# Context tiles normalized and turned during the second gated network's down product, and taken ahead of x by the first joint block

## The chip, the cores and the metric

The kernel runs on one core of a Trainium2 chip. The metric is the device time of one execution in microseconds, and the time of a kernel is the median of its runs. Engine names are those of the profile: PE is TensorE (PEld its weight loads), DVE VectorE, ACT ScalarE, POOL GpSimd, SP SyncE, which issues the loads of the weights.

## What is computed

`reference` is two blocks in a row on 256 tokens x 1024 features, all in float32. The first has two layers (a mixer, cross attention to a memory, and a gated feed-forward network each). The second has two joint layers: x (256 tokens) and a context (256 tokens) are each normalized and modulated, projected by one weight to queries, keys and values, and attend together; then a mixture of experts follows. The stretch that matters here is the end of the first block's second layer and the beginning of the second block's first:

```python
x = x + swiglu(rmsnorm(x, norm_ffn[l]), ffn_w_gu[l], ffn_w_down[l])     # l = 1
...
xc = ctx                                                                # not touched so far
mod  = (silu_c  @ w_ada[i] + b_ada[i])[:, None, :]                      # i = 0
modc = (silu_cc @ w_ada[i] + b_ada[i])[None, None, :]
sh_a, sc_a, ...  = jnp.split(mod, 6, axis=-1)
shc_a, scc_a, ... = jnp.split(modc, 6, axis=-1)
h  = _modulate(_rmsnorm(x,  g_attn[i]), sh_a,  sc_a)                    # 256 x 1024
hc = _modulate(_rmsnorm(xc, g_attn[i]), shc_a, scc_a)                   # 256 x 1024
q, k, v    = _split_qkv(h,  w_qkv[i])                                   # 1024 x 1536
qc, kc, vc = _split_qkv(hc, w_qkv[i])
```

So `hc` needs nothing of the first block, and `h` needs all of it.

## The kernel before

Each engine has its own program, written out by hand in the order in which it runs; semaphores tie them together. Nothing reorders it.

Tokens are cut into tiles of 128: tiles 0 and 1 are x, 2 and 3 the context (both in `xs`). A dense product goes in slots: one slot is a weight block of 1024 rows (8 pieces of 128; 6 in some slots of the down product) by 512 columns, kept in one of four ring buffers. Float32 is done in three products of a rounded format: both the activations and the weights are split into a high part and what is left (low part), and high x high, high x low and low x high are summed. Weight blocks are split by ACT (`split`, L1295, the high part into another ring buffer) and DVE (L1740, the low part in place), a slot ahead (`ahead`). A unit is one tile by one slot, 24 products of 128x512 into one PSUM bank (18 for a slot of six pieces). PE signals `w_used` as it begins a slot, and SP then issues the load that takes the buffer set free.

An activation tile is made ready by `norm`: DVE sums the squares (L1721), POOL raises the mean square to the power -0.5 (L2655), DVE multiplies by that and by the scale row in `bc` slot 0 (L1769) and adds the shift row of slot 1 (L1772) into `hb`; PE turns it with eight 128x128 transposes into banks T0 and T1 (L687), ACT copies each bank as the high part (L1280) and DVE subtracts for the low part (L1727). T0 and T1 must be free of that before the next tile is turned. The scale and shift rows are fetched by POOL (`fill`) from a scratch tensor that POOL's `modulation(0)` wrote in the linear attention; one fill has to wait until the rows before it in the same buffer were used (`normed`).

The down product of the gated network (`ff_out1`, within `feed_forward`) has six slots by two tiles: three slots into banks 0 and 1, three into banks 2 and 3. Its activations `ff_T` take the first 11264 columns of the 12288-column `arena`. Then `joint(0)` follows: two ada blocks (condition vector by modulation weights, L665, for the layer after), both x tiles and both context tiles normalized, with high parts in `hT` and low parts (`LO_J`) in the last 4096 columns of the arena; then slot 0 of `qkv0` on tiles 0, 1, 2, 3, slot 1 on the same, two more ada blocks, the turning of queries, and slot 2. ACT reads out the even tiles (L1376) and DVE the odd ones (L1920). The context itself was loaded by POOL in `cross(1)`.

## Time and profile before

| what | value |
|---|---|
| median of 3 runs | 2543.71 us (2541.72 to 2549.36) |
| the profiled execution | 2542.04 us, span 2540.2 us |
| PE busy | 2137.8 us, 84% of the span |
| DVE, ACT, POOL busy | 1087.4, 681.5, 262.3 us |
| mean granted clock of PE | 0.922 of full |

The page cuts the span in 40 slices of 63.5 us. Two expert stages (slices 21 to 29 and 32 to 40, roughly) have the DMA engines busy in nine tenths and DVE in one tenth; elsewhere PE is the busy one and DMA has room. The stretch between the end of the second gated network's up product (about 932 us) and the second pair of ada blocks in the joint layer (1067 us) lies in slices 15 to 17. In the timelines, a row merges instructions of one form that follow each other; its "idle before" is the time in which the engine did nothing ahead of it, with the instruction that ended it. In a table by stretch, a granted clock of 1.00 is 2.4 GHz and 0.50 is 1.2 GHz.

### The profile page before, as it was taken

To read this page: it belongs to the slowest core of one execution; us is meant where nothing else is said; L and a number is where in the kernel's file an instruction comes from. 1 tells how busy PE (TensorE), PEld (TensorE's weight loads), DVE (VectorE), ACT (ScalarE), POOL (GpSimd) and SP (SyncE) were. 2 spreads that over 40 slices of the span, in tenths; PEclk is the share of its full clock that TensorE was granted. 3 is DMA by queue.
4 is the path that set the end of the run, shared out by engine and by line. 5 is a ranking of instruction groups with operands and counts; after the bars stand their busy time and mean duration, and the time that the engine had idled before them with its cause. 6 is when DMAs were issued, how large, how long until landed. Compare 5 with 4: busy or idle time off the path is not lost. (4 is left out here: it accounts for less than half of the span.)

```text
span 2540.2 us, 29357 instructions
## 1 busy us (share of the span) xinstructions
PE 2137.8 (84%) x11338; PEld 1358.5 (53%) x11338; DVE 1087.4 (43%) x1713; ACT 681.5 (27%) x1048; POOL 262.3 (10%) x392
## 2 busy tenths in 40 slices
PE   6889999996999997987979888888568698888884
PEld 5777787784777876764733333333355433333331
DVE  5667644545676545467531111111576411111112
ACT  3343434332333432246211011111316111111111
POOL 2010000100000000000211111111120111111110
PEclk9989999997999998999979999999779799999997
DMA  8745565551655646310489999999810889999994
GB/s 278 266 144 203 181 211 191 202 200 67 236 199 182 217 173 216 110 35 1 189 354 396 409 413 406 410 404 382 276 25 1 311 356 408 422 415 413 413 414 188
DMA packets 175984, 655.24 MB, mean 258 GB/s; under 512 B 17680, under 2 KB 63200, under 8 KB 150544
## 3 DMA queue, kind: packets, MB, share of 16 engines
q1 hardware_dynamic: 157888, 618.45, 63.7%
q0 software_dynamic: 16752, 32.20, 3.9%
q10 hardware_dynamic: 1248, 3.25, 0.3%
q8 instruction: 68, 1.11, 0.2%
q14 instruction: 28, 0.23, 0.0%
HBM read 653.64 MB, written 21.17 MB: 266 GB/s over the span
## 5 line engine op out<-in xcount | busy, mean ns | idle before, releaser
L651 PE MATMUL bank<-sb_ring_rounded,sb_hT_rounded 128*128 128x512 f32 x2672 | 675.5, 397 | 18.9 <-DVE sb_hT_rounded L1727 12.2
L1185 PE MATMUL bank<-sb_ring,sb_arena 128*64 128x512 f32 x1984 | 507.4, 659 | 129.5 <-DMA sb_ring<-in_w_up 126.7
L651 PEld LDWEIGHTS bank<-sb_ring_rounded,sb_hT_rounded 128*128 128x128 f32 x2672 | 506.0, 191 | 128.5 <-DVE sb_hT_rounded L1727 14.1
L1740 DVE TENSOR_TENSOR sb_ring_rounded<-sb_ring,sb_ring_rounded 128x2048 fp32r<-128x2048 f32 (+1 forms) x148 | 328.2, 2259 | 133.1 <-ACT sb_ring_rounded L1295 132.8
L1185 PEld LDWEIGHTS bank<-sb_ring,sb_arena 128*64 128x64 f32 x1984 | 155.9, 150 | 426.4 <-issue 418.9
L1295 ACT ACTIVATE sb_ring_rounded<-sb_ring 128x2048 fp32r<-128x2048 f32 (+1 forms) x148 | 271.7, 1886 | 171.1 <-PE bank L651 141.8
L651 PE MATMUL bank<-sb_ring_rounded,sb_arena_rounded 128*128 128x512 f32 x1168 | 312.5, 393 | 2.0 <-DVE sb_arena_rounded L1727 1.0
L651 PEld LDWEIGHTS bank<-sb_ring_rounded,sb_arena_rounded 128*128 128x128 f32 x1168 | 221.1, 190 | 48.8 <-issue 2.6
L1209 PE MATMUL bank<-sb_ring,sb_arena 128*64 128x512 f32 x1024 | 233.7, 598 | 1.7 <-DVE sb_arena L2458 1.7
L1643 ACT ACTIVATE sb_hb<-bank 64x512 f32<-64x512 f32 x64 | 37.8, 590 | 644.6 <-PE bank L1185 644.6
L2458 DVE COPY sb_arena<-bank 128x256 f32<-128x256 f32 x64 | 27.2, 425 | 396.1 <-PE bank L1196 396.0
L2474 DVE COPY sb_arena<-bank 64x512 f32<-64x512 f32 x64 | 44.3, 693 | 231.0 <-PE bank L1185 231.0
L2464 DVE COPY sb_arena<-bank 64x512 f32<-64x512 f32 x64 | 44.3, 693 | 205.6 <-PE bank L1209 205.6
L1209 PEld LDWEIGHTS bank<-sb_ring,sb_arena 128*64 128x64 f32 x1024 | 68.4, 137 | 116.4 <-issue 110.4
L2607 POOL DMA_INDIRECT scratch_y<-sb_arena,sb_pick x64 | 60.2, 941 | 448.1 <-DVE sb_arena L2464 439.2
L1177 PEld LDWEIGHTS bank<-sb_cst,sb_arena 64*128 64x128 f32 x512 | 61.2, 199 | 68.9 <-issue 68.9
L687 PE MATMUL bank<-sb_cst,sb_hb 128*128 128x128 f32 x192 | 32.9, 326 | 74.2 <-DVE sb_hb L2539 22.3
L1634 ACT ACTIVATE sb_arena<-bank 64x512 f32<-64x512 f32 x64 | 37.8, 590 | 195.8 <-PE bank L1209 195.8
L1177 PE MATMUL bank<-sb_cst,sb_arena 64*128 64x64 f32 x512 | 70.0, 278 | 17.9 <-DMA sb_arena<-scratch_tokens,sb_spare 17.9
L2655 POOL TENSOR_TENSOR sb_st<-sb_st,sb_cst 128x1 f32<-128x1 f32 x32 | 28.6, 899 | 542.2 <-DVE sb_st L1722 446.2
L1280 ACT ACTIVATE sb_hT_rounded<-bank 128x512 fp32r<-128x512 f32 x68 | 38.9, 595 | 159.5 <-PE bank L687 156.3
L832 PE MATMUL bank<-sb_cst,sb_hb 128*128 128x128 f32 x320 | 48.9, 296 | 25.1 <-DVE sb_hb L1954 24.4
(315 smaller groups left out, 1955.0 us busy)
## 6 DMA issues: line engine op xcount, KB each, us to landing
sb_ring<-in_w_down SPq DMA_DIRECT2D x64, 2048.0 KB, 22.8
sb_ring<-in_w_up SPq DMA_DIRECT2D x62, 2048.0 KB, 21.8
sb_ring<-in_w_gate SPq DMA_DIRECT2D x62, 2048.0 KB, 17.5
sb_ring<-in_w_ada SPq DMA_DIRECT2D x48, 1024.0 KB, 7.4
sb_ring<-in_ffn_w_gu SPq DMA_DIRECT2D x44, 1024.0 KB, 7.7
sb_ring<-in_xa_w_kv SPq DMA_DIRECT2D x16, 1024.0 KB, 7.3
sb_ring<-in_ffn_w_down SPq DMA_DIRECT2D x16, 1024.0 KB, 6.4
sb_ring<-in_od_w_in SPq DMA_DIRECT2D x12, 1024.0 KB, 6.3
```

Source lines behind the costliest of these rows:

```text
L651: ins = pe.matmul(bank[b][0:rows, :], rnd(x), rnd(w[:, k, :]), start=start and k == k0 and q == 0, stop=stop and k == k1 - 1 and q == len( ...
L832: ins = pe.transpose(bank[T0 + a][:, k * P:(k + 1) * P], j_e[:, m % 2, a, k * P:(k + 1) * P], ident)
L1177: ins = pe.transpose(bank[T0 + j][:, k * ROWS:(k + 1) * ROWS], mx[0:ROWS, j, k:D:KD], ident[0:ROWS, 0:ROWS])
L1185: ins = pe.matmul(bank[2 * j + part][part * ROWS:(part + 1) * ROWS, :], mxT[:, j, k, :], w[:, k, :], start=k == 0, stop=k == KD - 1)
L1209: ins = pe.matmul(bank[S0 + n][n * ROWS:(n + 1) * ROWS, :], mactT[:, j, k, :], w[:, k, n * NB:(n + 1) * NB], start=k == 0, stop=k == 3)
L1280: act.activation(rnd(dst), bank[b][:, 0:n * P].rearrange("p (k n) -> p k n", k=n), ACT.Copy).then_inc(*c.up(s["x_hi"]))
L1295: act.activation(rnd(high_of(n)[:, k0:k1, :]), slot_of(n)[:, k0:k1, :], ACT.Copy).then_inc(*c.up(s["w_hi"]))
L1634: act.activation(my[0:ROWS, j, 0:NB], bank[S0][0:ROWS, :], ACT.Copy).then_inc(m["y_lo"], 1)
L1740: dve.tensor_tensor(rnd(w), w, whole(high_of(n)[:, k0:k1, :]), ALU.subtract).then_inc(*c.up(s["w_lo"]))
L2464: dve.tensor_copy(my[0:ROWS, j, NB:2 * NB], bank[S1][ROWS:P, :]).then_inc(m["y_hi"], 1)
L2474: dve.tensor_copy(mup[0:ROWS, j, :], bank[2 * j + 1][ROWS:P, :]).then_inc(m["up"], 1)
L2607: pool.indirect_dma_start(out=DR["y"][l], out_offset=bass.IndirectOffsetOnAxis(ap=pick[:, 1, j:j + 1], axis=0), in_=my[0:ROWS, j, :], in_o ...
```

## The change

Five things are done.

1. In the down product of layer 1, DVE normalizes both context tiles right behind its first weight split (`norm([2, 3], ..., turn=False)`), PE turns them behind the third slot (`norm(2)` in `feed_forward`), ACT copies their high parts ahead of its fourth further split, and DVE subtracts the low parts behind its two residual additions.
2. POOL fetches the context's scale and shift rows first and x's behind them.
3. The context's high parts now go to columns 0 and 1 of `hT`, its low parts to columns 2 and 3, and x's high and low parts to the arena's last 4096 columns (`HI_QKV0`, `LO_QKV0`), which are free only after the down product.
4. In `joint(0)` slot 0 takes the tiles in the order 2, 3, 0, 1, and x's tiles are turned ahead of its second and third unit. The banks read out follow that order.
5. The short row of sinks gets a semaphore of its own, `sink_loaded`, in place of sharing `ctx_loaded`.

The diff, without the hunk that adds `sink_loaded` to the list of semaphores:

```diff
...
@@ -409,9 +409,11 @@
 
         LO2 = (hT, 2)
         LO_J = (view(8192, 2, KD, 2 * P), 0)
+        HI_QKV0 = ((view(8192, KD, 2 * P), 0), (hT, -2))
+        LO_QKV0 = ((view(10240, KD, 2 * P), 0), (hT, 0))
 
         def low(lo, t, k0=0, k1=KD):
-            v, off = lo
+            v, off = lo[t // 2] if isinstance(lo[0], tuple) else lo
             if len(v.shape) == 4:
                 return v[:, t // 2, k0:k1, t % 2 * P:(t % 2 + 1) * P]
             return v[:, k0:min(k1, v.shape[1]), (off + t) * P:(off + t + 1) * P]
@@ -976,6 +978,8 @@
                         ins = unit(b, n0 + q, t, turned(0, q), turned(1, q), q % 3 == 0, q % 3 == 2)
                         if q % 3 == 2:
                             publish(ins, b, "d")
+                    if l == 1 and q == 2:
+                        norm(2)
                 if l == 0:
                     tile_by_tile(n0 + 4, lambda q: turned(0, q + 4), lambda q: turned(1, q + 4), False, ((2, 3), (2, 3)))
 
@@ -1064,13 +1068,19 @@
                 publish(ins, b, "d")
 
             def joint(l):
+                n0 = first[f"qkv{l}"]
                 if l == 0:
                     modulate("qkv0")
-                norm(2)
-                if l == 0:
+                    for u, t in enumerate((2, 3, 0, 1)):
+                        if u in (1, 2):
+                            norm_tile(u - 1)
+                        if u == 3:
+                            hT_settled()
+                        claim(u)
+                        publish(unit(u, n0, t, HI_QKV0, LO_QKV0), u, copy_by(0, t))
+                else:
                     norm(2)
-                hT_settled()
-                n0 = first[f"qkv{l}"]
+                    hT_settled()
 
                 def queries(tiles):
                     for t in tiles:
@@ -1082,10 +1092,10 @@
                         transpose_queries(jq[:, t, 0:D])
 
                 if l == 0:
-                    gemm(n0, 2, [0, 1, 2, 3], copy_by, LO_J)
+                    gemm(n0 + 1, 1, [0, 1, 2, 3], copy_by, LO_QKV0, hi=HI_QKV0)
                     modulate("qkv0_rest")
                     queries(range(4))
-                    gemm(n0 + 2, 1, [0, 1, 2, 3], copy_by, LO_J)
+                    gemm(n0 + 2, 1, [0, 1, 2, 3], copy_by, LO_QKV0, hi=HI_QKV0)
                 else:
                     gemm(n0, 2, [0, 1], copy_by, LO_J)
                     gemm(n0 + 2, 1, [0, 1], copy_by, LO_J)
@@ -1484,6 +1494,8 @@
                         high((T0, T1)[t], ff_T[:, 0, 2 * i:2 * i + 2, t * P:(t + 1) * P], 2)
                 c.next(s["mul_ready"], 2)
                 for q in range(4 if l == 0 else 6):
+                    if l == 1 and q == 3:
+                        norm([2, 3], HI_QKV0)
                     ahead(first[f"ff_out{l}"] + q)
                 if l == 0:
                     tile_by_tile(first["ff_out0"] + 4)
@@ -1540,15 +1552,14 @@
             def joint(l):
                 if l == 0:
                     modulated("qkv0")
-                norm([0, 1])
-                if l == 0:
-                    norm([2, 3])
+                    norm([0, 1], HI_QKV0)
                 else:
+                    norm([0, 1])
                     scale_rows([2, 3])
                 if l == 0:
                     ahead(first["qkv0"])
-                    for t in (0, 2):
-                        project(0, t, t)
+                    for t in (2, 0):
+                        project(0, t, 2 - t)
                     project(1, 0, 0)
                     flag(s["proj_act"])
                     ahead(first["qkv0"] + 1)
@@ -2142,7 +2153,12 @@
                 n0 = first[f"ff_out{l}"]
                 for q in range(3):
                     ahead(n0 + q)
+                    if l == 1 and q == 0:
+                        dve.wait_ge(s["ctx_loaded"], 16)
+                        norm([2, 3], 0, 1, turn=False)
                 residual(None, [(0, t) for t in range(2)])
+                if l == 1:
+                    turned([2, 3], LO_QKV0, HI_QKV0)
                 ahead(n0 + 3)
                 if l == 1:
                     ahead(n0 + 4)
@@ -2234,10 +2250,8 @@
 
             def joint(l):
                 if l == 0:
-                    norm([0, 1], 0, 1, lo=LO_J)
-
-                    dve.wait_ge(s["ctx_loaded"], 32)
-                    norm([2, 3], 0, 1, lo=LO_J)
+                    norm([0, 1], 0, 1, turn=False)
+                    turned([0, 1], LO_QKV0, HI_QKV0)
                 hbf = hb[:].rearrange("p a b -> p (a b)")
                 table = lambda at, t: cst[:, at + HD * t:at + HD * (t + 1)]
 
@@ -2260,13 +2274,14 @@
 
                 if l == 0:
                     ahead(first["qkv0"])
-                    for t in (1, 3):
-                        project(0, t, t)
+                    for t in (3, 1):
+                        project(0, t, 4 - t)
                     project(1, 1, 1)
                     settle()
                     dve.wait_ge(*c.next(s["proj_act"]))
                     for t in range(2):
                         turn_queries(t)
+                    dve.wait_ge(s["sink_loaded"], 16)
                     step(dve.tensor_scalar(nsink, sink1, -1.0, None, ALU.mult))
                     ahead(first["qkv0"] + 1)
                     project(1, 3, 3)
@@ -2738,18 +2753,16 @@
             for l in range(2):
 
                 if l == 0:
-                    fill(0, mod(l, 0, 1))
-                    fill(1, mod(l, 0, 0))
-                    norms()
-                else:
-                    norms()
+                    fill(0, mod(l, 1, 1))
+                    fill(1, mod(l, 1, 0))
+                norms()
                 if l == 0:
                     with nc.allow_non_contiguous_dma(reason="a short row"):
-                        pool.dma_start(sink1, I["sink_a_2"][0].partition_broadcast(P)).then_inc(s["ctx_loaded"], 16)
+                        pool.dma_start(sink1, I["sink_a_2"][0].partition_broadcast(P)).then_inc(s["sink_loaded"], 16)
                 fill(2, mod(l, 0, 2))
                 normed()
-                fill(0, mod(l, 1, 1))
-                fill(1, mod(l, 1, 0))
+                fill(0, mod(l, 1 - (l == 0), 1))
+                fill(1, mod(l, 1 - (l == 0), 0))
                 norms()
                 normed()
                 if l == 0:
```

How the order on DVE changes, from the second split of the down product on. Before: L1740 is a split, L1809 a residual addition, L1721 and L1722 the mean square, L1769 and L1772 the two steps of modulation.

```order
L1740 TENSOR_TENSOR sb_ring_rounded<-sb_ring,sb_ring_rounded 128x2048 x2
L1740 TENSOR_TENSOR sb_ring_rounded<-sb_ring,sb_ring_rounded 128x1536 x2
L1740 TENSOR_TENSOR sb_ring_rounded<-sb_ring,sb_ring_rounded 128x2048 x2
L1809 TENSOR_TENSOR sb_xs<-sb_xs,bank 128x512 x2
L1740 TENSOR_TENSOR sb_ring_rounded<-sb_ring,sb_ring_rounded 128x2048 x2
L1740 TENSOR_TENSOR sb_ring_rounded<-sb_ring,sb_ring_rounded 128x1536 x2
L1740 TENSOR_TENSOR sb_ring_rounded<-sb_ring,sb_ring_rounded 128x2048 x2
L1809 TENSOR_TENSOR sb_xs<-sb_xs,bank 128x512 x2
L1721 ISA sb_hb,sb_st<-sb_xs 128x1024
L1721 ISA sb_st 128x1
L1722 TENSOR_SCALAR sb_st<-sb_st 128x1
```

After, from the same place (the lines are 11 further down: L1751, L1820, L1732, L1733, L1780, L1783; L1738 is the subtraction):

```order
L1751 TENSOR_TENSOR sb_ring_rounded<-sb_ring,sb_ring_rounded 128x2048 x2
L1732 ISA sb_hb,sb_st<-sb_xs 128x1024
L1732 ISA sb_st 128x1
L1733 TENSOR_SCALAR sb_st<-sb_st 128x1
L1732 ISA sb_hb,sb_st<-sb_xs 128x1024
L1732 ISA sb_st 128x1
L1733 TENSOR_SCALAR sb_st<-sb_st 128x1
L1780 SCALAR_TENSOR_TENSOR sb_hb<-sb_xs,sb_st,sb_bc 128x1024
L1783 TENSOR_TENSOR sb_hb<-sb_hb,sb_bc 128x1024
L1780 SCALAR_TENSOR_TENSOR sb_hb<-sb_xs,sb_st,sb_bc 128x1024
L1783 TENSOR_TENSOR sb_hb<-sb_hb,sb_bc 128x1024
L1751 TENSOR_TENSOR sb_ring_rounded<-sb_ring,sb_ring_rounded 128x1536 x2
```

Further down on DVE, after:

```order
L1751 TENSOR_TENSOR sb_ring_rounded<-sb_ring,sb_ring_rounded 128x2048 x2
L1820 TENSOR_TENSOR sb_xs<-sb_xs,bank 128x512 x2
L1738 TENSOR_TENSOR sb_hT_rounded<-bank,sb_hT_rounded 128x4x128 x4
L1751 TENSOR_TENSOR sb_ring_rounded<-sb_ring,sb_ring_rounded 128x2048 x2
L1751 TENSOR_TENSOR sb_ring_rounded<-sb_ring,sb_ring_rounded 128x1536 x2
L1751 TENSOR_TENSOR sb_ring_rounded<-sb_ring,sb_ring_rounded 128x2048 x2
L1820 TENSOR_TENSOR sb_xs<-sb_xs,bank 128x512 x2
L1732 ISA sb_hb,sb_st<-sb_xs 128x1024
```

The ten rows of the context's normalization have moved from behind the down product and x's tiles to a place behind the first split, and its four subtractions stand behind the first pair of residual additions.

How the order on PE changes, from the last transposes of the up product to the first slot of the projection. Before: L954 turns the gated activations, L651 is a product, L665 an ada block, L687 a transpose. From the last rows shown on, pairs and single products go on alternating, since high and low parts lie in different tensors.

```order
L954 MATMUL bank<-sb_cst,sb_arena 128x128 x4
L651 MATMUL bank<-sb_ring_rounded,sb_arena_rounded 128x512 x264
L665 MATMUL bank<-sb_ring,sb_silu 32x128 x64
L687 MATMUL bank<-sb_cst,sb_hb 128x128 x32
L651 MATMUL bank<-sb_ring_rounded,sb_hT_rounded 128x512 x2
L651 MATMUL bank<-sb_ring_rounded,sb_arena_rounded 128x512
L651 MATMUL bank<-sb_ring_rounded,sb_hT_rounded 128x512 x2
L651 MATMUL bank<-sb_ring_rounded,sb_arena_rounded 128x512
```

After (L956, L653, L667, L689 are the same four):

```order
L956 MATMUL bank<-sb_cst,sb_arena 128x128 x4
L653 MATMUL bank<-sb_ring_rounded,sb_arena_rounded 128x512 x132
L689 MATMUL bank<-sb_cst,sb_hb 128x128 x16
L653 MATMUL bank<-sb_ring_rounded,sb_arena_rounded 128x512 x132
L667 MATMUL bank<-sb_ring,sb_silu 32x128 x64
L653 MATMUL bank<-sb_ring_rounded,sb_hT_rounded 128x512 x24
L689 MATMUL bank<-sb_cst,sb_hb 128x128 x8
L653 MATMUL bank<-sb_ring_rounded,sb_hT_rounded 128x512 x24
L689 MATMUL bank<-sb_cst,sb_hb 128x128 x8
L653 MATMUL bank<-sb_ring_rounded,sb_arena_rounded 128x512 x96
L653 MATMUL bank<-sb_ring_rounded,sb_hT_rounded 128x512 x48
L667 MATMUL bank<-sb_ring,sb_silu 32x128 x64
```

Of the 32 transposes that stood between the ada blocks and the projection, 16 stand in the middle of the down product's 264 products, and eight each behind the first and the second unit of the projection.

## Rows read from the trace of the kernel before

**Rows 1.** By stretch: its us, then each engine's busy us, granted clock, DMA.

```profile
997.60:1022.20 24.60, 6.96 (x33) 5.61 (x33) 17.71 (x22) 5.79 (x10) 8.25 (x16) 0.58 0.66 238
1022.20:1025.50 3.30, 3.30 (x8) 2.63 (x9) 2.31 (x2) 2.75 (x2) 2.57 (x6) 0.50 0.46 96
1025.50:1067.40 41.90, 41.90 (x186) 34.43 (x184) 14.09 (x15) 6.52 (x8) 0.00 (x0) 1.00 0.26 94
```

**Rows 2.** Timeline of PE: start, us, line, what, count, idle before.

```profile
932.25 61.70 PE L651 MATMUL bank<-sb_ring_rounded,sb_arena_rounded 128*128 128x512 f32 x264 [0.98 <-issue]
993.89 3.70 PE L665 MATMUL bank<-sb_ring,sb_silu 128*32 128x128 f32 x128
1000.42 1.09 PE L687 MATMUL bank<-sb_cst,sb_hb 128*128 128x128 f32 x8 [2.84 <-DVE sb_hb L1772]
1003.57 1.94 PE L687 MATMUL bank<-sb_cst,sb_hb 128*128 128x128 f32 x8 [2.05 <-DVE sb_arena_rounded L1727]
1015.63 1.97 PE L687 MATMUL bank<-sb_cst,sb_hb 128*128 128x128 f32 x8 [10.12 <-DVE sb_hb L1772]
...
1022.18 1.19 PE L651 MATMUL bank<-sb_ring_rounded,sb_hT_rounded 128*128 128x512 f32 x2 [1.46 <-DVE sb_arena_rounded L1727]
...
1067.43 3.70 PE L665 MATMUL bank<-sb_ring,sb_silu 128*32 128x128 f32 x128
```

**Rows 3.** Timeline of DVE, same columns, down product to projection.

```profile
934.77 4.50 DVE L1740 TENSOR_TENSOR sb_ring_rounded<-sb_ring,sb_ring_rounded 128x2048 fp32r<-128x2048 f32 x2 [2.62 <-ACT sb_ring_rounded L1295]
946.78 3.43 DVE L1740 TENSOR_TENSOR sb_ring_rounded<-sb_ring,sb_ring_rounded 128x1536 fp32r<-128x1536 f32 x2 [7.51 <-ACT sb_ring_rounded L1295]
...
988.01 4.49 DVE L1740 TENSOR_TENSOR sb_ring_rounded<-sb_ring,sb_ring_rounded 128x2048 fp32r<-128x2048 f32 x2 [7.88 <-ACT sb_ring_rounded L1295]
...
994.72 1.23 DVE L1721 CUSTOM_DVE_ANT_0 sb_hb<-sb_xs 128x1024 f32<-128x1024 f32 x1
...
1001.60 1.22 DVE L1772 TENSOR_TENSOR sb_hb<-sb_hb,sb_bc 128x1024 f32<-128x1024 f32 x1
...
1023.19 4.49 DVE L1740 TENSOR_TENSOR sb_ring_rounded<-sb_ring,sb_ring_rounded 128x2048 fp32r<-128x2048 f32 x2 [1.11 <-ACT sb_ring_rounded L1295]
```

**Rows 4.** Timeline of POOL, first layer's modulation rows and powers.

```profile
802.90 1.12 POOL L2649 DMA_DIRECT2D sb_bc<-scratch_mod  x2 [1.62 <-DVE sb_hb L1819]
...
1003.12 1.05 POOL L2649 DMA_DIRECT2D sb_bc<-scratch_mod  x2 [3.83 <-DVE sb_hb L1772]
```

**Rows 5.** Timeline of ACT, projection's read-outs and weight split.

```profile
1021.25 3.70 ACT L1295 ACTIVATE sb_ring_rounded<-sb_ring 128x2048 fp32r<-128x2048 f32 x2
...
1040.34 0.60 ACT L1376 ACTIVATE sb_arena<-bank 128x512 f32<-128x512 f32 x1 [10.28 <-PE bank L651]
1051.22 0.60 ACT L1376 ACTIVATE sb_arena<-bank 128x512 f32<-128x512 f32 x1 [10.28 <-PE bank L651]
```

**Rows 6.** Timeline of PE, two earlier places with transposes among products.

```profile
156.48 1.03 PE L687 MATMUL bank<-sb_cst,sb_hb 128*128 128x128 f32 x8
158.58 1.17 PE L687 MATMUL bank<-sb_cst,sb_hb 128*128 128x128 f32 x8 [1.07 <-DVE sb_arena_rounded L1727]
159.50 11.14 PE L651 MATMUL bank<-sb_ring_rounded,sb_hT_rounded 128*128 128x512 f32 x48
...
288.74 1.03 PE L687 MATMUL bank<-sb_cst,sb_hb 128*128 128x128 f32 x8
289.52 10.69 PE L651 MATMUL bank<-sb_ring_rounded,sb_hT_rounded 128*128 128x512 f32 x46
```

**Rows 7.** Loads into the ring between 990 and 1050 us, its last line.

```profile
DMA to landing us min/median/max: 5.2/7.4/16.4
```

**Rows 8.** What SP waited for, 940 to 1330 us: total, times, longest.

```profile
SPq L545 <- PE bank L651: 164.0, 1, 164.0
```

**Rows 9.** Table by stretch as in rows 1, at two places of gaps.

```profile
156.40:159.50 3.10, 2.03 (x19) 1.63 (x16) 1.98 (x3) 1.34 (x3) 0.00 (x0) 1.00 0.00 0
...
934.00:936.00 2.00, 2.00 (x6) 1.57 (x5) 1.23 (x1) 2.00 (x2) 0.00 (x0) 0.50 0.77 270
```

More of the change, by code:

```diff
@@ L175, in build_program @@
             "act_back", "act_go", "act_step", "ctx_loaded", "bcx", "o_split", "dve_step", "e_ready",
-            "es_ready", "fin_ready", "gla_dve", "h_ready", "idx_ready", "logits_read", "in_loaded",
+            "es_ready", "fin_ready", "gla_dve", "h_ready", "idx_ready", "logits_read", "sink_loaded", "in_loaded",
             "marks_ready", "fix_loaded", "mem_loaded", "mod_stored", "raw_stored0", "raw_stored1", "silu_ready", "ms_ready", "mul_ready", "nmax_ready", "out_done",
```

## The prediction

> **What bounds the kernel now.** I read the 40 slices of the page first: up to the first expert stage (about 1270 us) TensorE is busy in eight or nine tenths of nearly every slice while the DMA engines are half idle; in the expert stages the picture is turned round. The changed stretch, 930 to 1100 us, lies in the part that TensorE sets. A table by stage then shows how it is filled [rows 1]: the down product of the gated network and the ada blocks stand without a gap [rows 2], and then 24.60 us follow in which PE works 6.96 us, at a granted clock of 0.58. After it PE is full again, first at 0.50 of its clock, then at 1.00. The timeline of PE names the hole [rows 2]: the last product ends at 993.89, two ada blocks take 3.70 us, then 32 transposes stand in pairs of eight, the first three behind idle times of 2.84, 2.05 and 10.12 us, and the first product of the joint projection starts at 1022.18. Every idle time there is put down to DVE, which normalizes x, turns it, and then does both again for the context.
>
> The timeline of POOL says why 10.12 us are the longest: the context's scale and shift rows are fetched into the buffers that x's rows still fill, so their transfers start at 1003.12, only when x is normalized [rows 4], and after landing and modulation the context's first transpose stands at 1015.63 [rows 2]. The context's own data have been in place since the second cross attention. So the hole depends on order, not on late data.
>
> **What is removed.** I count PE's time from the end of the down product (993.89) to the start of the next ada blocks (1067.43), the same two points of work in both kernels: 73.54 us now [rows 2]. Between them lie 8 units of 24 products. ACT reads every second unit out at 1040.34 and 1051.22, so two units take 10.88 us and one 5.44 at full clock [rows 5]; 8 are 43.52. Now they take 1067.43 - 1022.18 = 45.25, because they begin at half clock.
>
> **What stands there after the change.**
> Two ada blocks: 3.70, unchanged [rows 2].
> Two units on context tiles follow, the first at once, since the context was turned before. Their weights are split by DVE at 988.01 to 992.50 [rows 3], about 8 us before they are wanted, and this moves with PE.
> x's tile 0: now PE could begin to transpose it 1000.42 - 993.89 = 6.53 us after the last product [rows 2]; wanted after 3.70 + 5.44 = 9.14. Covered by 2.6 us. Tile 1 is normalized at 1002.8 (end of the row at 1001.60 [rows 3]), 8.9 us after the last product, wanted at 15.4. Covered by 6.4.
> Each x tile still costs its 8 transposes on PE. Where eight transposes stand in front of products that don't need them, PE goes on after 289.52 - 288.74 = 0.78 us [rows 6]: twice 0.78 is 1.56. Copy and subtraction of the first half are done 158.58 - 156.48 = 2.1 us after the first transpose [rows 6] and lie beside a unit of 5.44.
> Sum from 993.89's point of work: 3.70 + 43.52 + 1.56 = 48.78 us, instead of 73.54: 24.76 us less.
>
> **What is added.** 16 transposes of the context in the down product, behind its third slot (at about 963.9 us), where PE has no gap now. The nearest row is a pair of eight between products at full clock: 156.48 to 159.50, 3.02 us, 1.07 of it idle because the second tile's bank is freed by DVE's subtraction [rows 6]. Lower bound: no wait, 2 x 0.78 = 1.56. Upper bound: the same pair in the hole, 1000.42 to 1005.51, 5.1 us [rows 2]. I take 3.1, the row at full clock with products on either side; DVE is in its last residual addition when the first half is turned, but ACT's copy hides that. ACT does its four copies before the next weight split. That split and DVE's own, 3.70 and 4.50 us by a first and second half that overlap, follow from about 967.5 to 974; PE wants them one slot of 10.88 us after 967.0, at 977.9. Nothing follows from it.
> The context's normalization costs DVE 994.72 to 1002.8, 8.1 us [rows 3]. It is put behind the split that ends at 939.27, so it ends at 947.4; DVE is idle now until 946.78. The split of the 1536-wide piece slips 0.6 us, to end at 950.8. PE wants it at about 955.8: back from 993.9 over slots of 8.16, 10.88 and 10.88 us to 963.9, and 8.16 more. What stands behind the new wait for the context on DVE is this split, and PE behind it; the wait is empty, as POOL issued the rows at 802.90 [rows 4], and POOL itself has nothing in front of its power. Its queue of fills moves with that: x's rows are issued at about 947 and land far ahead of 997.
> The next split (second slot of the projection) is what becomes late next. Now: started by ACT at 1021.25 and done by DVE at 1027.7 [rows 3, 5], 18 us early. Afterwards: ACT is free when it has copied x's tile 1, (993.89 + 3.1) + 3.70 + 5.44 + 0.78 + 5.44 + about 2.2 = 1014.6; DVE's first half ends at 1018.8 and the second at 1021.1; PE wants the first at 997.0 + 3.70 + 21.76 + 1.56 = 1024.0. Covered by 5 us. The weights for it are issued when PE begins the first ada block, then at about 997.4; the slowest load into the ring between 990 and 1050 landed in 16.4 us [rows 7], so by 1013.8, before ACT asks. The slot after it keeps its distance from its load, which PE releases as it begins the second slot.
> The other edits (sink on its own semaphore, other slot numbers of banks) change no duration; the bank order only swaps which of two free banks is read first. I cost them at 0, with 0.3 either way.
>
> **Sum:** 24.76 - 3.1 = 21.7 us. Later stages start when PE arrives: SP's first expert load waits 164.0 us for PE's product [rows 8], and so do the loads before it, so the whole rest moves up. The profiled execution took 2542.04 us (span 2540.20); 2542.04 - 21.7 = 2520.3. It lies 1.7 us below the median 2543.71, which would give 2522.0. I forecast 2522.
>
> **The clock.** At 156.4 to 159.5, eight and eight transposes between products, the granted clock stays 1.00 [rows 9]. But soon after 932.25, behind an idle time of 0.98 us, it is 0.50 [rows 2, 9], and the 264 products take 61.70 us [rows 2] where 59.84 would do (264 x 10.88 / 48): 1.9 us lost. So a fall at the new place is possible and costs up to 1.9 us.
> The Trainium skill (TensorE: Matmul & The Clock Gate, Part 4: PE-mode transpose) says that transposes don't count as work for the clock the way products do. By that rule a fall at the inserted transposes would be the usual case and the forecast 2524; by this trace's row at 156.4 it is the exception.
>
> **Rivals.**
> (a) The clock falls once or twice more, at 964 or at x's tiles: 1.9 to 3.8 us back, 2523.9 to 2525.8. For: 932.2. Against: 156.4 and 288.74, where products went on at full speed.
> (b) A wait takes the hole's place: the second slot's split or x's tile 0 comes later than worked out. x's tile 0 has only 2.6 us of cover. If POOL's answer or x's rows were 5 us later, PE would stand 2.4 us; if the load of the second slot shared its rate with both ada loads and took twice 16.4 us, it would land at 1030, ACT's first half and DVE's be done 4.1 us later at 1034, 10 us late: 2532. Against: all are earlier in every row.
> (c) The gain is given back in the expert stage: if its loads ran at a fixed rate from a fixed moment, nothing of 21.7 us would be left, 2543.7. Against it stands rows 8: the loads start at PE's release.
> (d) Slower than before: the clock falls at the inserted transposes at 964 and stays at 1.2 GHz to the end of the down product. The remaining products take 993.89 - 963.9 = 30.0 us at full clock and 60 at half: +30.0 - 21.7, 2552. It decides from the point where more than 21.7 us worth of products run at half clock. Against: behind the hole, with a gap ten times as long as the one added, the half clock lasted from 1022.2 to 1025.5 only [rows 1].
> The same page (Part 1, Seeing it yourself) warns of clocks seen stuck low for tens of microseconds; no row here shows it.
> (e) The change does not do what it says: the context's rows are not there at 939 and DVE waits. They were issued 136 us before.
>
> **How the numbers follow.** Forecast as worked out 0.71; (a) 0.17; (b) 0.07; (c) and (e) together 0.03; (d) 0.02. The time given is the first's, 2522. Its own range is 2517 to 2526 (1.5 less and 2.0 more for the inserted pair, and the three runs of before spread 7.6 us). To take in (a) and part of (b): 2515 to 2530. A difference of 0.3%, 7.6 us, is about what can be told from none. Forecast, (a) and most of (b) are faster by more, (c) and (e) same, (d) slower: 0.95, 0.03, 0.02.
>
> **What would show it.** Right: 16 transposes at about 964 with some 3 us to the next product; products of the joint projection right behind the ada blocks, about 997.0 + 3.7; two pieces of eight transposes without idle time; no idle time on PE near 10 us there; the second pair of ada blocks starting at about 1045.7 (1067.43 - 21.7). Wrong: an idle time before x's tile 0 above 0.5 us, PE waiting for the weight split at about 1024, a clock of 0.50 after 967, or expert loads that start less than some 21.7 us earlier than now.

## The result and the profile after

| | before | after |
|---|---|---|
| median of 4 runs | 2545.32 us (2541.72 to 2549.36) | 2523.91 us (2520.56 to 2526.08) |
| the profiled execution | 2542.04 us, span 2540.2 | 2525.83 us, span 2524.0 |
| PE busy | 2137.8 us | 2135.7 us |
| start of the down product | 932.25 | 936.72 |
| from there to the second pair of ada blocks | 135.18 | 113.96 |
| from there to the first expert load | 168.02 | 164.30 |
| from there to the end | 1304.75 | 1309.02 |

The ratio is 0.9915, its 95% interval 0.9898 to 0.9932: a gain of 0.7 to 1.0%, clear of none. (The median of before has four runs here; the table ahead of the prediction had three of them.) The median fell by 21.4 us; 21.7 was forecast. Of the four stretches in the table the second is the one that the change touches, and it gave 21.22 us. The other three differ by +4.47, -3.72 and +4.27 us, so that the two profiled executions lie only 16.2 us apart; they are taken up below.

The timeline of PE after the change, with the columns of [rows 2]:

```profile
936.72 31.79 PE L653 MATMUL bank<-sb_ring_rounded,sb_arena_rounded 128*128 128x512 f32 x132 [0.98 <-issue]
968.35 1.04 PE L689 MATMUL bank<-sb_cst,sb_hb 128*128 128x128 f32 x8
970.46 1.16 PE L689 MATMUL bank<-sb_cst,sb_hb 128*128 128x128 f32 x8 [1.07 <-DVE sb_hT_rounded L1738]
971.38 30.18 PE L653 MATMUL bank<-sb_ring_rounded,sb_arena_rounded 128*128 128x512 f32 x132
1001.49 3.70 PE L667 MATMUL bank<-sb_ring,sb_silu 128*32 128x128 f32 x128
1005.12 5.74 PE L653 MATMUL bank<-sb_ring_rounded,sb_hT_rounded 128*128 128x512 f32 x24
1010.70 1.03 PE L689 MATMUL bank<-sb_cst,sb_hb 128*128 128x128 f32 x8
1011.49 5.71 PE L653 MATMUL bank<-sb_ring_rounded,sb_hT_rounded 128*128 128x512 f32 x24
1017.03 1.04 PE L689 MATMUL bank<-sb_cst,sb_hb 128*128 128x128 f32 x8
1017.83 22.05 PE L653 MATMUL bank<-sb_ring_rounded,sb_arena_rounded 128*128 128x512 f32 x96
1039.71 11.04 PE L653 MATMUL bank<-sb_ring_rounded,sb_hT_rounded 128*128 128x512 f32 x48
1050.68 3.70 PE L667 MATMUL bank<-sb_ring,sb_silu 128*32 128x128 f32 x128
```

The transposes of the context stand at 968.35, and 3.03 us later the products go on. Behind the two ada blocks the first unit of the projection begins at once, at 1005.12, where [rows 2] had 24.6 us of transposes and idle time. The two x tiles are the rows of eight at 1010.70 and 1017.03, each 0.79 or 0.80 us ahead of the next product and without idle time. No row between the inserted pair and the second ada pair has an idle time in brackets. The table by stretch, answering to [rows 1], shows PE full and its clock at full speed in each of its four windows between 968 and 1046 us, but for the 1.07 us in which PE waits at the inserted pair:

```profile
968.00:997.00 29.00, 27.93 (x132) 23.09 (x131) 12.57 (x10) 12.03 (x10) 0.00 (x0) 1.00 0.48 166
1001.00:1006.00 5.00, 5.00 (x135) 4.32 (x134) 3.94 (x8) 0.56 (x2) 1.99 (x2) 1.00 0.54 169
1006.00:1024.00 18.00, 18.00 (x89) 15.06 (x88) 10.33 (x10) 6.68 (x8) 6.09 (x13) 1.00 0.92 339
1024.00:1046.00 22.00, 22.00 (x99) 18.22 (x98) 8.36 (x10) 5.33 (x7) 0.00 (x0) 1.00 0.27 95
```

The timeline of DVE gives the normalization of the context (first and last row), the split that had to wait for it, the end of x's tile 0 and the split of the second slot:

```profile
943.88 1.22 DVE L1732 CUSTOM_DVE_ANT_0 sb_hb<-sb_xs 128x1024 f32<-128x1024 f32 x1
...
950.76 1.23 DVE L1783 TENSOR_TENSOR sb_hb<-sb_hb,sb_bc 128x1024 f32<-128x1024 f32 x1
951.90 3.42 DVE L1751 TENSOR_TENSOR sb_ring_rounded<-sb_ring,sb_ring_rounded 128x1536 fp32r<-128x1536 f32 x2
...
1006.74 1.22 DVE L1783 TENSOR_TENSOR sb_hb<-sb_hb,sb_bc 128x1024 f32<-128x1024 f32 x1
...
1020.59 4.49 DVE L1751 TENSOR_TENSOR sb_ring_rounded<-sb_ring,sb_ring_rounded 128x2048 fp32r<-128x2048 f32 x2 [1.01 <-ACT sb_ring_rounded L1305]
```

The context is ready at 951.99; the split of the 1536-wide piece starts as the last step ends, and is done at 955.32, about 5 us before PE begins that slot (968.35 less the 8.16 us of a slot of six pieces). x's tile 0 is ready at 1007.96 and PE asks for it at 1010.70. The split ends at 1025.08, while PE's fifth unit starts at about 1028.8 (1039.71 less two units of 5.44). The next two views are ACT's splits of the second and the third slot, the latter with a wait of 1.75 us for its load (1.90 in the kernel before), and POOL's power and fetch of x's rows:

```profile
1018.64 3.73 ACT L1305 ACTIVATE sb_ring_rounded<-sb_ring 128x2048 fp32r<-128x2048 f32 x2
...
1037.06 3.72 ACT L1305 ACTIVATE sb_ring_rounded<-sb_ring 128x2048 fp32r<-128x2048 f32 x2 [1.75 <-DMA sb_ring<-in_w_qkv]
```

```profile
945.39 1.99 POOL L2670 TENSOR_TENSOR sb_st<-sb_st,sb_cst 128x1 f32<-128x1 f32 x2 [136.88 <-DVE sb_st L1733]
...
952.28 1.05 POOL L2664 DMA_DIRECT2D sb_bc<-scratch_mod  x2 [3.83 <-DVE sb_hb L1783]
```

### The profile page after: what moved, and what is told of

Its sections match the earlier page's. It is cut to its first block and busy times, and to the rows that moved or that the text cites. A ratio compares the mean times of both kernels' runs of the same rounds, so it can differ in the third digit from the quotient of the medians.

```text
span 2524.0 us, 29358 instructions
## 1 busy us (share of the span) xinstructions
PE 2135.7 (85%) x11338; PEld 1357.3 (54%) x11338; DVE 1086.6 (43%) x1713; ACT 681.3 (27%) x1048; POOL 262.4 (10%) x392
## 5 line engine op out<-in xcount | busy, mean ns | idle before, releaser
L653 PE MATMUL bank<-sb_ring_rounded,sb_hT_rounded 128*128 128x512 f32 x2624 | 650.6, 398 | 17.4 <-DVE sb_hT_rounded L1738 12.2
L653 PEld LDWEIGHTS bank<-sb_ring_rounded,sb_hT_rounded 128*128 128x128 f32 x2624 | 497.5, 192 | 125.6 <-DVE sb_hT_rounded L1738 14.1
L1751 DVE TENSOR_TENSOR sb_ring_rounded<-sb_ring,sb_ring_rounded 128x2048 fp32r<-128x2048 f32 (+1 forms) x148 | 328.1, 2258 | 125.9 <-ACT sb_ring_rounded L1305 125.6
L653 PE MATMUL bank<-sb_ring_rounded,sb_arena_rounded 128*128 128x512 f32 x1216 | 308.9, 393 | 2.0 <-issue 2.0
L653 PEld LDWEIGHTS bank<-sb_ring_rounded,sb_arena_rounded 128*128 128x128 f32 x1216 | 229.9, 190 | 50.6 <-issue 2.6
L689 PE MATMUL bank<-sb_cst,sb_hb 128*128 128x128 f32 x192 | 30.2, 307 | 60.4 <-DVE sb_hb L2554 23.5
```

Of the source, the lines that this page charges most:

```text
L653: ins = pe.matmul(bank[b][0:rows, :], rnd(x), rnd(w[:, k, :]), start=start and k == k0 and q == 0, stop=stop and k == k1 - 1 and q == len( ...
L1751: dve.tensor_tensor(rnd(w), w, whole(high_of(n)[:, k0:k1, :]), ALU.subtract).then_inc(*c.up(s["w_lo"]))
```

## The experiments

Each cut of a diff below shows the part of the edit that matters; what has to follow it on the other engines (copies, subtractions, the order in which banks are read out) is left out.

All comparisons of stages use the stretch from the down product's first product to the second pair of ada blocks, called the stretch. It is read from the traces; its spread for one kernel is 0.05 us for three traces after the change (113.96, 114.01, 113.96) and 0.3 for four before (135.18, 135.50, 135.34, 135.46; what varies is the landing of the context's rows, with PE waits of 10.12 to 10.60 us). Medians of whole runs spread far more, as the last two parts show.

**The two halves of the change.** `x_first` keeps the early context and undoes the order of slot 0:

```diff
-                    for u, t in enumerate((2, 3, 0, 1)):
-                        if u in (1, 2):
-                            norm_tile(u - 1)
-                        if u == 3:
-                            hT_settled()
+                    norm(2)
+                    hT_settled()
+                    for u, t in enumerate((0, 1, 2, 3)):
```

> The changed kernel, but slot 0 of the joint projection takes x's tiles first and the context's behind them, both x tiles being turned ahead of the first unit, as before the change. The context is still normalized and turned in the down product. Theory (two things make the gain, the early context and the order of the tiles, which hides x's normalization and turning behind units on context tiles): PE waits for x's tile 0 until 6.5 us after the last product, turns the pair in 5.1, waits 1.5 more: first product 13.1 us after the last one instead of 3.6, less 1.6 for the transposes saved between units, 7.9 us more than the changed kernel, and up to 1.9 more if the clock falls: 2532 to 2534. Rival (the hole was above all the 10 us wait for the context's rows, so that the early context alone brings nearly all): within 3 us of the changed kernel, 2524 to 2527.

Measured: the stretch 123.92 us, median 2531.66 (2530.68 to 2536.72; ratio to before 0.9946, 0.9925 to 0.9968). PE's timeline there, and the clock of the first products behind it:

```profile
1001.14 3.70 PE L667 MATMUL bank<-sb_ring,sb_silu 128*32 128x128 f32 x128
1007.67 1.09 PE L689 MATMUL bank<-sb_cst,sb_hb 128*128 128x128 f32 x8 [2.83 <-DVE sb_hb L1781]
1010.82 1.94 PE L689 MATMUL bank<-sb_cst,sb_hb 128*128 128x128 f32 x8 [2.06 <-DVE sb_arena_rounded L1736]
1014.22 13.52 PE L653 MATMUL bank<-sb_ring_rounded,sb_arena_rounded 128*128 128x512 f32 x48 [1.46 <-DVE sb_arena_rounded L1736]
```

```profile
1014.20:1017.00 2.80, 2.78 (x7) 2.22 (x8) 1.78 (x1) 2.79 (x2) 2.60 (x6) 0.50 0.82 229
```

PE waits 2.83, 2.06 and 1.46 us, the clock falls to 0.50, and the 48 products of x's tiles, a row of 13.52 us, take 2.4 us more than a row of 48 at full clock (11.1). The first product stands 13.08 us after the first ada block instead of 3.63, less 1.59 for the two rows of eight that the changed kernel has between units: 7.9 us of waiting and transposing. The other 2.1 us are in the eight units, 46.08 us here and 43.97 in the changed kernel, and come with the lower clock. The stretch is 9.96 us longer than the changed kernel's; 7.9 to 9.8 was expected. The rival is out.

`ctx_late` undoes the early context and keeps the order (beside the turning in the joint block, as in `turn_late` below):

```diff
-                    if l == 1 and q == 0:
-                        dve.wait_ge(s["ctx_loaded"], 16)
-                        norm([2, 3], 0, 1, turn=False)
...
                 if l == 0:
+                    dve.wait_ge(s["ctx_loaded"], 16)
+                    norm([2, 3], 0, 1, turn=False)
+                    turned([2, 3], LO_QKV0, HI_QKV0)
                     norm([0, 1], 0, 1, turn=False)
```

> The changed kernel without the early context: it is normalized and turned in the joint block, ahead of x, and slot 0 still takes the context's tiles first. With the kernel that had the early context but x first, this makes a square of two by two. Theory (the two parts overlap, since each hides a piece of the same hole): the context's tile 0 is ready 6.5 us after the last product, the pair of transposes ends at 11.6, the first product stands there; x's scale and shift rows are fetched behind the context's normalization and land about 19 us after the last product, so that PE waits some 3 us for x's tile 0; the second pair of ada blocks starts about 61.4 us after the last product. That makes 123.1 us from the start of the down product, 12.1 less than before and 9.1 more than the changed kernel. Order alone is then worth 12, the early context alone 11.3 (the kernel with x first: 123.9 us), both together 21.2. Rival (the parts add up without overlap, order alone 21.2 - 11.3 = 9.9): 125.3 us.

Measured: the stretch 124.56 us, median 2532.33 (2530.41 to 2536.24; ratio 0.9943, 0.9922 to 0.9965).

```profile
1005.94 1.40 PE L689 MATMUL bank<-sb_cst,sb_hb 128*128 128x128 f32 x8 [3.30 <-DVE sb_hb L1781]
1009.09 1.94 PE L689 MATMUL bank<-sb_cst,sb_hb 128*128 128x128 f32 x8 [1.75 <-DVE sb_hT_rounded L1736]
1010.68 6.98 PE L653 MATMUL bank<-sb_ring_rounded,sb_hT_rounded 128*128 128x512 f32 x24
1020.17 1.95 PE L689 MATMUL bank<-sb_cst,sb_hb 128*128 128x128 f32 x8 [2.51 <-DVE sb_hb L1781]
1021.77 6.59 PE L653 MATMUL bank<-sb_ring_rounded,sb_hT_rounded 128*128 128x512 f32 x24
```

The waits came where expected, 3.30 us for the context and 2.51 for x. But the two units took 6.98 and 6.59 us instead of 5.7. Behind each gap and its transposes the granted clock was down, at the start of either unit, and the expectation had left this out:

```profile
1010.60:1012.00 1.40, 1.40 (x6) 1.21 (x5) 0.99 (x2) 0.81 (x2) 0.00 (x0) 0.50 1.00 369
1021.80:1024.00 2.20, 2.20 (x8) 1.76 (x7) 1.97 (x3) 0.69 (x2) 0.99 (x3) 0.58 0.22 85
```

So the square reads, against the mean of 135.37 before: early context alone 11.45 us, order alone 10.81, both 21.4. The parts add up to 22.3, so they overlap by 0.9 us, where the theory had 2.1 and the rival none. The measured 124.56 lies between the 123.1 of the theory and the 125.3 of the rival, nearer to the rival; since 2.1 us of it are slow units that neither had, it does not decide between them. What the square does show is that each part hides about half of the hole: the context's normalization goes behind the down product, x's behind units on context tiles.

**Where the context is turned.** `turn_late` moves its transposes, copies and subtractions behind the first pair of ada blocks:

```diff
-                    if l == 1 and q == 2:
-                        norm(2)
...
+                    norm(2)
                     for u, t in enumerate((2, 3, 0, 1)):
```

> The changed kernel, but the context, normalized early as in it, is turned in the joint block, between the first pair of ada blocks and slot 0, not in the down product. Theory (the transposes cost PE the same 3.0 us anywhere, and what counts is what waits behind them): 3.0 us move from the down product to the joint block, and DVE can only begin x's normalization when the context is turned out of the shared buffer, 8.4 us after the last product instead of 0.8, so x's tile 0 comes at 14.0 where it is wanted at 12.2: 1.9 us more than the changed kernel, 115.9 us in the stretch. Rival (the transposes disturb the down product beyond their own time, by its splits or loads): the stretch gets shorter than 113.9 us.

Measured: the stretch 114.96 us, median 2525.26 (2523.91 to 2526.30; ratio 0.9913, 0.9894 to 0.9932).

```profile
935.61 60.09 PE L653 MATMUL bank<-sb_ring_rounded,sb_arena_rounded 128*128 128x512 f32 x264 [0.98 <-issue]
995.63 3.70 PE L667 MATMUL bank<-sb_ring,sb_silu 128*32 128x128 f32 x128
999.26 1.09 PE L689 MATMUL bank<-sb_cst,sb_hb 128*128 128x128 f32 x8
1002.22 1.16 PE L689 MATMUL bank<-sb_cst,sb_hb 128*128 128x128 f32 x8 [1.87 <-DVE sb_hT_rounded L1736]
1003.14 5.73 PE L653 MATMUL bank<-sb_ring_rounded,sb_hT_rounded 128*128 128x512 f32 x24
1010.55 1.09 PE L689 MATMUL bank<-sb_cst,sb_hb 128*128 128x128 f32 x8 [1.68 <-DVE sb_hb L1781]
```

The stretch as a whole misleads: here the down product took 60.02 us for its 264 products, against 61.6 to 61.9 in every other trace, since its first products ran at full clock in this execution (granted clock 1.00, where the others show 0.50 from 1.5 to 3 us behind the first product). From the ada blocks on it is 54.94 us; the changed kernel has 49.19 there and 3.03 for its pair ahead. So turning late costs 2.7 us, 1.9 expected: 1.68 us of wait for x's tile 0, and a pair that takes 3.88 us instead of 3.03. ACT stores the ada rows ahead of its copy there and takes the first half 1.50 us after the first transpose, instead of 0.64. The rival, that the transposes disturb the down product, finds nothing: with the pair taken out, the two rows of 132 products in the changed kernel make 31.63 + 30.11 = 61.74 us, and `before` has 61.64.

**What an interruption costs.** `turn_apart` turns the two context tiles behind different slots:

```diff
-                    if l == 1 and q == 2:
-                        norm(2)
+                    if l == 1 and q in (2, 3):
+                        norm_tile(q - 2)
```

> The changed kernel, but the two context tiles are turned apart: tile 2 behind the third slot of the down product, tile 3 behind the fourth. Theory (the inserted pair costs 3.03 us because the second tile waits 1.07 us for its bank to be freed; eight transposes between products that do not need them cost 0.79): 2 x 0.79 = 1.58 us instead of 3.03, so 1.45 us less than the changed kernel, 2522.5, and no idle time on PE between 968 and 1001 us. Rival (each interruption of the product stream has its own price, such as a drained pipeline or a fall of the clock): two interruptions cost as much as one pair or more, 2524 to 2526.

```profile
963.47 1.04 PE L689 MATMUL bank<-sb_cst,sb_hb 128*128 128x128 f32 x8
964.27 11.14 PE L653 MATMUL bank<-sb_ring_rounded,sb_arena_rounded 128*128 128x512 f32 x48
975.24 1.03 PE L689 MATMUL bank<-sb_cst,sb_hb 128*128 128x128 f32 x8
976.03 19.30 PE L653 MATMUL bank<-sb_ring_rounded,sb_arena_rounded 128*128 128x512 f32 x84
```

Each eight cost 0.79 or 0.80 us, without idle time. The stretch is 112.65 us, 1.3 less than the changed kernel. The rival is out. The median was 2520.49 (2517.95 to 2526.32; ratio 0.9900, 0.9881 to 0.9919), in the same set in which the changed kernel had 2519.08; this says nothing of 1.3 us. So it was run again:

> The kernel with the two context tiles turned apart, beside the changed kernel on one chip. Theory (1.4 us less in the down product, and nothing else): 112.6 us in the stretch, and a median 0 to 3 us below the changed kernel's, which so many runs can hardly tell. Rival (the second interruption costs as much as it saves): 114.0 us in the stretch.

The stretch was 112.64 us again, the median 2523.41 (2522.59 to 2526.46; ratio 0.9917, 0.9904 to 0.9931) beside the changed kernel's 2523.44. It is the better kernel by its trace in the stretch; in the whole time the step is too small to be seen.

`turn_five` repeats each of the inserted transposes:

```diff
-                    for k in range(4):
+                    for k in list(range(4)) * times:
...
-                        norm(2)
+                        norm(2, times=5)
```

> The changed kernel, but each of the 16 transposes inserted in the down product is done five times into the same place, 64 more, 80 in a row without a product among them. Theory (transposes in a dense row keep the granted clock at 1.00, and time spent on PE in the down product goes one to one into the end): 80 x 0.099 = 7.9 us between the products instead of 3.03, the wait for the bank being covered, so 4.9 us more than the changed kernel, 2528.8, the granted clock 1.00 behind them. Rival 1 (transposes do not count as work for the clock, so a long row of them makes it fall): the products behind them begin at 0.50 and 1.5 to 3.5 us more are lost, 2530.3 to 2532. Rival 2 (time before the joint block is absorbed later): no difference to the changed kernel, 2524.

Measured: the stretch 119.63 us, median 2526.67 (2524.27 to 2533.44; ratio 0.9925, 0.9902 to 0.9949).

```profile
967.07 8.90 PE L689 MATMUL bank<-sb_cst,sb_hb 128*128 128x128 f32 x80
975.73 30.17 PE L653 MATMUL bank<-sb_ring_rounded,sb_arena_rounded 128*128 128x512 f32 x132
```

```profile
967.00:976.00 9.00, 9.00 (x83) 8.93 (x81) 2.77 (x4) 1.79 (x3) 0.00 (x0) 1.00 0.00 0
976.00:980.00 4.00, 4.00 (x19) 3.29 (x19) 2.25 (x2) 3.99 (x3) 0.00 (x0) 1.00 0.61 189
```

80 transposes take 8.66 us, 0.108 each, a little more than the 0.099 expected, and 5.63 us more than the pair of 3.03. The stretch grew by 5.65. The granted clock is 1.00 in them and behind them, and the 132 products that follow take 30.10 us as in the changed kernel (30.11). So a dense row of transposes did not bring the clock down in this trace, and rival 1 is out for a row of this length. The Trainium skill (TensorE: Matmul & The Clock Gate, Part 4: PE-mode transpose) says that the full clock doesn't engage for transposes, since they don't count as work in the same way; this trace does not bear that out for 8.66 us that began at full clock. Where the clock did fall, PE had waited: it was down behind the gaps of `x_first` (2.83, 2.06 and 1.46 us) and of `ctx_late` (3.30, 1.75 and 2.51). It stayed at 1.00 behind those of `turn_late` (1.87 and 1.68) and of `x_together` (1.07 and 1.52). In all of these transposes stand beside the gaps, so no run here tells how much is due to the gaps alone. Rival 2 is out as well.

`x_together` turns both x tiles ahead of the third unit:

```diff
-                        if u in (1, 2):
-                            norm_tile(u - 1)
-                        if u == 3:
+                        if u == 2:
+                            norm(2)
                             hT_settled()
```

> The changed kernel, but both x tiles are turned together ahead of the third unit, instead of one tile each ahead of the second and the third. Theory (a tile's copy and subtraction are free only where a unit on another tile stands behind its transposes): the pair costs 2.1 + 0.8 us and then 1.5 us until its last half is subtracted, 4.4 instead of 1.58, so 2.9 us more than the changed kernel, 116.9 us in the stretch from the start of the down product. Rival (PE's queue hides it, only the transposes themselves cost): 113.9 to 114.3 us.

Measured: the stretch 117.07 us, 3.1 more than the changed kernel (2.9 expected), median 2529.45 (2524.22 to 2530.38; ratio 0.9931, 0.9913 to 0.9950).

```profile
1011.55 1.03 PE L689 MATMUL bank<-sb_cst,sb_hb 128*128 128x128 f32 x8
1013.66 1.16 PE L689 MATMUL bank<-sb_cst,sb_hb 128*128 128x128 f32 x8 [1.07 <-DVE sb_arena_rounded L1737]
1016.34 22.03 PE L653 MATMUL bank<-sb_ring_rounded,sb_arena_rounded 128*128 128x512 f32 x96 [1.52 <-DVE sb_arena_rounded L1737]
```

The pair takes 2.1 us to its second half and the third unit waits 1.52 us more for the last subtraction. Interleaving the tiles with units is what hides this. The rival, that only the transposes themselves cost, is out.

**Repeats, and the other stretches.**

> The changed kernel once more, for a second trace and a closer interval. Theory (the gain is the hole between down product and joint projection, 21.3 us there by the traces, and later stages only move up): median 21 to 22 us below before's; from the third product row of the down product to the second pair of ada blocks again 113.9 to 114.1 us. Rival (part of the gain sits in later stages, such as the attention that took 3.7 us less in the changed kernel's first trace, and part was lost in the expert stages, 4.3 us more): these two differences come back in the second trace with the same sign and size. By the theory they are chance and move by some us.

> The kernel before once more, for a second trace. Theory (the change acts only between the start of the down product and the second pair of ada blocks): that stretch takes 135.2 us again, within 0.3, while the stretches ahead of it (932 us) and from the second pair of ada blocks to the first expert load (168.0 us) move by some us of themselves, as the granted clock falls at other gaps. Rival (the attention stage of the changed kernel is 3.7 us shorter by the change): 168.0 us within 0.3 here too.

> The kernel before, for a third trace. Open so far: the time fell by 21.4 us in one set of runs and by 27.2 in another, the stretch from the down product to the second pair of ada blocks by 21.2 to 21.5. From the second pair of ada blocks to the first expert load, before took 168.0 and 167.6 us, the changed kernel 164.3 and 164.4, and six kernels with the same instructions there 164.7 to 168.5. Theory 1 (chance of the granted clock): before too shows values down to 164 to 166 in further traces. Theory 2 (entering the attention out of a dense row spares a fall of the clock): before stays at 167.5 or more.

> The kernel before, for a fourth trace: as for the third. Theory 1: somewhere between 164 and 168.5 us from the second pair of ada blocks to the first expert load; theory 2: 167.5 or more again.

> The changed kernel, for a third trace and more runs. From the down product to the second pair of ada blocks 114.0 us. From there to the first expert load: theory 1, somewhere between 164 and 168.5; theory 2, 164.5 or less again. The median difference to before: 21 to 22 by theory 1, since chance evens out; 24 to 25 by theory 2.

| kernel | down product starts | the stretch | to the first expert load | to the end |
|---|---|---|---|---|
| before | 932.25 | 135.18 | 168.02 | 1304.75 |
| before_again | 937.03 | 135.50 | 167.61 | 1304.76 |
| before_third | 931.39 | 135.34 | 164.30 | 1304.67 |
| before_fourth | 931.35 | 135.46 | 167.23 | 1305.76 |
| after | 936.72 | 113.96 | 164.30 | 1309.02 |
| after_again | 936.02 | 114.01 | 164.36 | 1306.11 |
| after_third | 937.21 | 113.96 | 164.90 | 1305.53 |
| x_first | 936.38 | 123.92 | 164.96 | 1304.54 |
| turn_apart | 931.81 | 112.65 | 166.58 | 1307.66 |
| turn_apart_again | 939.62 | 112.64 | 166.74 | 1304.50 |
| turn_five | 935.40 | 119.63 | 166.52 | 1304.45 |
| ctx_late | 937.27 | 124.56 | 164.72 | 1304.75 |
| turn_late | 935.61 | 114.96 | 167.59 | 1305.84 |
| x_together | 932.10 | 117.07 | 168.54 | 1304.69 |

The 4.5 us by which the changed kernel began the down product later are no loss of the change: the instructions ahead of it are the same in all rows, and the start lies anywhere from 931.35 to 939.62. The 3.7 us in the attention are no gain of it that can be shown: before has 164.30 too, in its third trace, as chance (theory 1) would have it and theory 2 not, and `turn_apart`, which differs from the changed kernel only in the down product, has 166.58 and 166.74. Yet the changed kernel's three (164.30, 164.36, 164.90) are all low against before's other three (168.02, 167.61, 167.23), and so few traces don't exclude a us or two. The 4.3 us of the expert stages did not come back: the two repeats have 1306.11 and 1305.53.

In whole runs: `after_again` had 2519.08 (2517.54 to 2522.34) beside 2546.23 for before, ratio 0.9889 (0.9870 to 0.9909), a difference of 27.2 us; `after_third` 2523.44 (2517.36 to 2525.62) beside 2545.01, ratio 0.9911 (0.9895 to 0.9928), 21.6 us. The single runs of `before_again`, `before_third` and `before_fourth` took 2546.67, 2537.54 and 2541.62. For both repeats 21 to 22 us were expected. Two of the three differences, 21.4 and 21.6, fit the 21.4 of the stretch; that of `after_again`, 27.2, does not, and why it is 6 us wider stays open. Its own interval reaches down to 23 us, and the two repeats ran on different chips, whose part in it no run here shows.

## Why the prediction was right

**The hole and what takes its place.** From the first ada block to the second pair: 48.78 us worked out, 49.19 measured (1050.68 - 1001.49). About 0.24 of the 0.4 us are in the first two units, 5.58 and 5.54 instead of 5.44, and 0.21 in the other six together (1017.83 to 1050.68, 32.85 us instead of 32.64). So 24.35 us were removed where 24.76 were worked out.

**The inserted pair.** 3.1 taken, 3.03 measured, with the same 1.07 us of idle time as in [rows 6]. The whole down product grew by 3.13 us (64.77 instead of 61.64), and 24.35 less 3.13 is the 21.22 us of the stretch. The lower bound of 1.56 was real: `turn_apart` reaches it with 0.80 and 0.79 us. The upper, 5.1, is what a pair took in the hole, and no inserted pair came near it.

**x's tiles.** Tile 0 was ready 6.5 us after the last product and wanted 9.2 after it (1007.96 and 1010.70): 2.7 us of cover, 2.6 worked out. Rival (b) did not happen, but it is close by: in `turn_late` DVE begins x 8 us later and PE waits 1.68 us.

**The next split.** It ended 3.7 us before PE's fifth unit; about 3 was worked out for its end. The split behind the context's normalization ended about 5 us before PE wanted it, as worked out (950.8 and 955.8), and cost PE nothing.

**The clock.** The granted clock was 1.00 at the inserted pair in all five traces that have it (`after` three times, `x_first`, `x_together`), so rivals (a) and (d) did not come, and `turn_five` speaks against their mechanism at a dense row of transposes. It does not test an idle gap as long as 2 us at this place.

**Later stages.** They start when PE arrives: lengthening the stretch by 10.0 us in `x_first` moved the first expert load from 1214.98 to 1225.26, and the part behind that load is 1304.45 to 1309.02 us in all 14 traces. Rival (c) is out. One sign of being wrong was a first expert load that comes less than some 21.7 us earlier. It came 20.47 us earlier (1235.45 and 1214.98), and the missing us is in stretches that the change does not touch: 21.22 of the stretch, less 4.47 ahead of it, and 3.72 in the attention.

**What was luck.** The mechanism and its terms are borne out by the stretch. That the two medians differ by 21.4 us, within 0.3 of the forecast, is closer than such runs can tell: the interval of this difference is about 17 to 26 us, a repeat gave 27.2, and the two profiled executions gave 16.2.

**What was mis-sized.** In the expectations, not in the sum: behind gaps where the clock falls, a gap costs more than its length. `ctx_late` lost 2.1 us on two such units, and this is what its expectation lacked.

## What to carry to other kernels

Where an input does not depend on the stage before, prepare it inside that stage, and let the first weight block begin with it: the work on the other input then hides behind its products. Turn tiles one at a time with a unit on another tile behind each, since eight transposes cost 0.8 us that way, and a pair in a row cost 1.3 us more than two apart in the down product and 3.1 us more ahead of a unit that needs them. A change of 1 us in a kernel whose runs spread by up to 9 us is seen in the stretch of the trace that it touches, measured between the same two instructions, and not in the median.

## What the runs showed of the hardware

The same instructions ahead of the down product took 931.35 to 939.62 us in 14 executions, and behind the same two gaps at its start (1.14 and 0.98 us) the clock fell to 0.50 within the first products in 13 of them and stayed at 1.00 in one (60.02 us for the 264 products against 61.6 to 61.9, transposes between them taken out). So the same gaps brought the clock down in most executions and not in all. Eighty transposes in a row, 8.66 us, left it at 1.00.
